# Up products of a split-float MLP: high weights times high and low features in one 512-column matmul

## The reference

```python
def sq_relu_mlp(h, w_up, w_down):
    return jnp.square(jax.nn.relu(h @ w_up)) @ w_down
# x = x + sq_relu_mlp(rms_norm_2(x, norm2_g[l]), w_up[l], w_down[l])
```

## Time and profile before

| | |
|---|---|
| median of 3 runs | 1287.84 us (1287.81 to 1287.95) |
| span of the profiled execution | 1285.7 us; the page gives no other time for it |
| TensorE busy | 1157.5 us, 90% |
| VectorE, ScalarE, GpSimd busy | 71%, 39%, 26% |
| up stage | about 1095 to 1194 us of the span |
| down stage | about 1194 to 1282 us of the span |

### The profile page before, as it was taken

The page is one execution under the profiler, slowest core; times in us unless marked ns, Lnnn a source line. Parts: engine busy times, 40 slices in busy tenths (PEclk is TensorE's granted clock), DMA queues, the critical chain, the costliest instruction groups (busy, mean ns, idle before and its releaser), DMA issues.

```text
span 1285.7 us, 15477 instructions
## 1 busy us (share of the span) xinstructions
PE 1157.5 (90%) x5466; PEld 822.4 (64%) x5466; DVE 911.5 (71%) x1879; ACT 504.7 (39%) x975; POOL 331.6 (26%) x311
## 2 busy tenths in 40 slices
PE   5899999999799998997888888788789999999998
PEld 5888999999755544442333433333335887999787
DVE  6875797788678777776777767677756786666544
ACT  4556544455432223212222122221514577555432
POOL 4000000000245545454444444535441000000000
PEclk9999999999899999999899989988999999999999
DMA  8854377686899999999999999999997523345550
GB/s 361 314 220 174 132 259 282 234 340 251 322 412 423 426 425 425 426 426 426 427 426 427 426 426 426 426 426 427 427 427 307 193 99 118 146 168 190 200 196 34
DMA packets 57697, 405.68 MB, mean 316 GB/s; under 512 B 6908, under 2 KB 7108, under 8 KB 9108
## 3 DMA queue, kind: packets, MB, share of 16 engines
q0 software_dynamic: 38576, 272.49, 50.6%
q1 hardware_dynamic: 19044, 132.19, 27.3%
HBM read 403.61 MB, written 1.05 MB: 315 GB/s over the span
## 4 chain that ended last, share of the span: by engine, by line
PE 47%; DMA 29%; DVE 13%; ACT 6%; issue 3%; POOL 1%; SPq 0%; DVEq 0%; POOLq 0%; ACTq 0%
DMA gbuf<-in_peer_uv,ei 16%; DMA ring<-in_peer_uv,ei 11%; PE bank L822 11%; PE bank L483 5%; PE bank L479 5%; PE bank L480 5%; DVE half L1501 4%; ACT half L1034 3%; PE bank L754 3%; PE bank L1008 2%; PE bank L1010 2%; PE bank L1009 2%; DMA row_place<-in_peer_uv,ei 1%; PE bank L500 1%; PE bank L494 1%
## 5 line engine op out<-in xcount | busy, mean ns | idle before, releaser
L822 PE MATMUL bank<-gbuf,dg 128*128 128x512 f32 x540 | 259.0, 625 | 49.2 <-ACT dg L1313 49.2
L1501 DVE TENSOR_TENSOR half<-ring,half 128x1024 fp32r<-128x1024 f32 x175 | 212.6, 1222 | 112.9 <-ACT half L1034 112.5
L822 PEld LDWEIGHTS bank<-gbuf,dg 128*128 128x128 f32 x540 | 105.1, 199 | 189.8 <-issue 120.3
L1944 DVE CUSTOM_DVE_ANT_0 gbuf<-gbuf,h2t 128x1024 f32<-128x1024 f32 x135 | 165.3, 1225 | 80.5 <-DMA gbuf<-in_peer_uv,ei 79.4
L1034 ACT ACTIVATE half<-ring 128x1024 fp32r<-128x1024 f32 x175 | 183.0, 1052 | 92.4 <-PE bank L1010 45.6
L2289 POOL DMA_INDIRECT gbuf<-in_peer_uv,ei x135 | 160.1, 1186 | 187.1 <-PE bank L822 110.7
L822 PE MATMUL bank<-ring,dg 128*128 128x512 f32 x356 | 171.4, 619 | 26.6 <-ACT dg L1313 26.6
L1305 ACT ACTIVATE za<-za 128x4 f32<-128x4 f32 x62 | 12.7, 205 | 399.6 <-DVE za L1944 399.6
L2289 POOL DMA_INDIRECT ring<-in_peer_uv,ei x89 | 106.8, 1200 | 166.1 <-DVE ei L1917 70.7
L1944 DVE CUSTOM_DVE_ANT_0 ring<-ring,h2t 128x1024 f32<-128x1024 f32 x89 | 108.9, 1225 | 54.7 <-DMA ring<-in_peer_uv,ei 54.7
L822 PEld LDWEIGHTS bank<-ring,dg 128*128 128x128 f32 x356 | 68.7, 196 | 116.6 <-issue 79.0
(11 more groups left out here) (440 smaller groups left out, 1962.2 us busy)
## 6 DMA issues: line engine op xcount, KB each, us to landing
ring<-in_weights SPq DMA_DIRECT2D x114, 1024.0 KB, 4.9
gbuf<-in_weights SPq DMA_DIRECT2D x4, 1024.0 KB, 9.7
gbuf<-in_peer_uv,ei POOLq DMA_INDIRECT x135, 23.2
wq_place<-in_weights SPq DMA_DIRECT2D x2, 1024.0 KB, 6.1
bcs<-in_b_ada POOLq DMA_DIRECT2D x3, 512.0 KB, 9.1
ring<-in_peer_uv,ei POOLq DMA_INDIRECT x89, 22.7
xs<-in_x SPq DMA_DIRECT2D x2, 512.0 KB, 8.4
ya<-in_weights SPq DMA_DIRECT2D x1, 1024.0 KB, 17.2
```

Of the source, the lines that this page charges most:

```text
L822: r = e.matmul(acc[a][j][:, :], dg[:, i % 4, :], expert_rows(i)[:, 1024 + 512 * j:1536 + 512 * j], start=h == 0 and k == 0, stop=h == 7 an ...
L1501: e.tensor_tensor(l, v, h.bitcast(f32), ALU.subtract).then_inc(*o.inc(s_lov, split(n)))
L1944: e.tensor_tensor_reduce(row, row, h2t[:, ITS[n][0], :], 1.0, 0.0, ALU.mult, ALU.add, za[:, n % 2, i % 16:i % 16 + 1]).then_inc(*o.inc(s_d ...
```

## The change

The high and the low features become two planes of one tensor `hf2`, so that both can be streamed behind each other: one matmul of 512 columns writes high x high into columns 0 to 255 of a bank and high x low into columns 256 to 511. The low weights still meet the high features alone, added to columns 0 to 255. All 32 blocks now go through `up_rows`. VectorE adds the two halves of the bank with a reduction over the pair (t, t + 256) and writes the sum to `rl`. ScalarE takes the relu of it in place, in SBUF, and then squares twice: into a new float32 buffer `rq` and, rounded, into `gh`. VectorE's low part is now `rq` minus `gh`. A bank is free after VectorE's sum.

```diff
-    hfh = feats.enter_context(nc.sbuf_tensor("hfh", [128, 8, T], f32r))
-    hfl = feats.enter_context(nc.sbuf_tensor("hfl", [128, 8, T], f32r))
+    hf2 = feats.enter_context(nc.sbuf_tensor("hf2", [128, 2, 8, T], f32r))
...
+    hfh, hfl = hf2[:, 0, :, :], hf2[:, 1, :, :]
...
-        def up_rows(f, g):
-            n = chunk_at["up", f]
+        def up_rows(f, k0, k1):
+
+            n, pb = chunk_at["up", f], banks[f % 4]
             hi, lo = high_done(n)
-            pb = bank(f)
-            for k in range(4 * g, 4 * g + 4):
-                for a in range(2):
-                    e.wait_ge(s_fhi, FHI["h4", 2 * a + g])
-                    e.wait_ge(s_flv, FLV["h4", 2 * a + g])
-                e.matmul(pb[:, 0:256], hi[:, k, :], hfh[:, k, :], start=k == 0, stop=False)
-                e.matmul(pb[:, 0:256], hi[:, k, :], hfl[:, k, :], start=False, stop=False)
+            for k in range(k0, k1):
+                if f < 2:
+                    for a in range(2):
+                        e.wait_ge(s_fhi, FHI["h4", 2 * a + k // 4])
+                        e.wait_ge(s_flv, FLV["h4", 2 * a + k // 4])
+                e.matmul(pb[:, :], hi[:, k, :], hf2[:, :, k, :], start=k == 0, stop=False)
             e.wait_ge(s_lov, split(n))
-            for k in range(4 * g, 4 * g + 4):
+            for k in range(k0, k1):
                 r = e.matmul(pb[:, 0:256], lo[:, k, :], hfh[:, k, :], start=False, stop=k == 7)
             return r
...
         for g in range(2, 32):
-            product("up", g, g % 4, hfh, hfl)
-            frees[g % 4] = ((s_relu, g + 1),)
+            if g < 4:
+                bank(g)
+            else:
+                e.wait_ge(s_usum, g - 3)
+            up_rows(g, 0, 8).then_inc(*o.inc(s_chunk, chunk_at["up", g] + 1))
...
         for g in range(32):
-            taken("up", g)
+            for m in ahead(chunk_at["up", g]):
+                hi(m)
+            e.wait_ge(s_usum, g + 1)
+            e.activation(rl[:, g % 3, :], rl[:, g % 3, :], AF.Relu).then_inc(*o.inc(s_relu, g + 1))
             if g >= 3:
                 e.wait_ge(s_flp, FLP["g", g - 3])
-            e.activation(rl[:, g % 3, :], banks[g % 4][:, 0:256], AF.Relu).then_inc(*o.inc(s_relu, g + 1))
-            e.wait_ge(s_gsq, 5 + g)
-            e.activation(gh[:, g, :], rl[:, g % 3, :], AF.Copy).then_inc(*o.inc(s_fhi, FHI["g", g]))
+            e.wait_ge(s_relu, g + 1)
+            e.activation(rq[:, g % 3, :], rl[:, g % 3, :], AF.Square).then_inc(*o.inc())
+            e.activation(gh[:, g, :], rl[:, g % 3, :], AF.Square).then_inc(*o.inc(s_fhi, FHI["g", g]))
...
-            e.tensor_tensor(gl_[:, g, :], rl[:, g % 3, :], gh[:, g, :].bitcast(f32), ALU.subtract).then_inc(
+            e.tensor_tensor(gl_[:, g, :], rq[:, g % 3, :], gh[:, g, :].bitcast(f32), ALU.subtract).then_inc(
                 *o.inc(s_flp, FLP["g", g]))
...
             lo(chunk_at["up", g] + 2)
-            e.wait_ge(s_relu, g + 1)
-            e.tensor_tensor(rl[:, g % 3, :], rl[:, g % 3, :], rl[:, g % 3, :], ALU.mult).then_inc(*o.inc(s_gsq, 5 + g))
+            if g >= 3:
+                e.wait_ge(s_fhi, FHI["g", g - 3])
+            e.wait_ge(s_chunk, chunk_at["up", g] + 1)
+            e.tensor_reduce(rl[:, g % 3, :], banks[g % 4][:, :].rearrange("p (j t) -> p t j", j=2), AX.X, ALU.add).then_inc(
+                *o.inc(s_usum, g + 1))
             if g:
                 square_lo(g - 1)
```

More of the change, by code:

```diff
@@ L173, in build_program @@
         "a2", "lru_in", "gl", "lru_mul", "g_sq", "xo", "neg_max", "norm_bcast_read", "h2_done", "h_gained", "rstd_diag", "first_experts")]
+    s_usum = sem("s_up_sum")
     s_pool, s_flp, s_id, s_const, s_wbd, s_iu = [sem("s_" + n) for n in (
@@ L351, in build_program @@
     rl = st("rl", [128, 3, T])
+    rq = st("rq", [128, 3, T])
     stage.close()
     ctx.push(feats)
+    hfh, hfl = hf2[:, 0, :, :], hf2[:, 1, :, :]
     bada, n1pre, ca_w, cqk_w = pc0[:, 8:56], pc0[:, 56:64], pc0[:, 64:88], pc0[:, 88:120]
@@ L970, in tensor_program @@
                 frees[2 * c + a] = ((s_gsq, 2 * c + a + 1),)
-        def up_rows(f, g):
-            n = chunk_at["up", f]
+        def up_rows(f, k0, k1):
+            n, pb = chunk_at["up", f], banks[f % 4]
             hi, lo = high_done(n)
-            pb = bank(f)
-            for k in range(4 * g, 4 * g + 4):
-                for a in range(2):
-                    e.wait_ge(s_fhi, FHI["h4", 2 * a + g])
-                    e.wait_ge(s_flv, FLV["h4", 2 * a + g])
-                e.matmul(pb[:, 0:256], hi[:, k, :], hfh[:, k, :], start=k == 0, stop=False)
-                e.matmul(pb[:, 0:256], hi[:, k, :], hfl[:, k, :], start=False, stop=False)
+            for k in range(k0, k1):
[4 more added lines that the diff above has]
+                e.matmul(pb[:, :], hi[:, k, :], hf2[:, :, k, :], start=k == 0, stop=False)
             e.wait_ge(s_lov, split(n))
-            for k in range(4 * g, 4 * g + 4):
+            for k in range(k0, k1):
                 r = e.matmul(pb[:, 0:256], lo[:, k, :], hfh[:, k, :], start=False, stop=k == 7)
             return r
-        up_rows(0, 0)
+        bank(0)
+        up_rows(0, 0, 4)
         for a in range(2):
             tokens_columns(a, 1)
-        up_rows(1, 0)
+        bank(1)
+        up_rows(1, 0, 4)
         for f in range(2):
-            up_rows(f, 1).then_inc(*o.inc(s_chunk, chunk_at["up", f] + 1))
-            frees[f] = ((s_relu, f + 1),)
+            up_rows(f, 4, 8).then_inc(*o.inc(s_chunk, chunk_at["up", f] + 1))
         for g in range(2, 32):
-            product("up", g, g % 4, hfh, hfl)
-            frees[g % 4] = ((s_relu, g + 1),)
+            if g < 4:
[3 more added lines that the diff above has]
+            up_rows(g, 0, 8).then_inc(*o.inc(s_chunk, chunk_at["up", g] + 1))
         accs = [bank(4 + i) for i in range(4)]
```

## The result

The changed kernel takes 1322.14 us (median of 4 runs, 1321.73 to 1322.32), the one before 1287.89 beside it: ratio 1.0267, 95% interval 1.0255 to 1.028. The forecast was 1321.3 us, in a range from 1315 to 1330.

What follows compares the result with a forecast made beforehand. The prediction took the ScalarE-VectorE ring, not TensorE, to bound the up stage: 31 x 1.06 + 0.6 = 33.5 us, and 1285.7 + 33.5 + 2.1 = 1321.3 us, 2.6% slower, range 1315 to 1330.

Steps and rivals of the forecast that it cites:

- the ring: Up stage, ScalarE and VectorE waiting on each other through splits, sum, relu and squares: 4.05 us a block, before 2.99.
- TensorE sets the pace after all: Rival, up stage: TensorE bounds it, a block goes from 2.99 to 2.8 us, 1282 us in all; chance 0.03.
- TensorE's saving is off the path: Up stage: wider matmuls make TensorE's block 2.8 us, saving at most 3 us, none of it on the path.
- The sum: VectorE's reduction of a bank's two halves, up stage: 0.69 us, time going with the 512 floats read.
- both rivals on it (0.42, 1.23): Sum priced by its 256 results, 0.42 us, 1312.7 us, chance 0.04; strided sum dear, 1.23 us, 1338.6 us, chance 0.08.
- Squares: ScalarE's Square to rq and Square to gh in the up stage: 0.33 us each from start to next start.
- Relu and its wait: ScalarE's relu from SBUF and the wait for its own result, up stage: 0.45 us together, moved into the ring.
- The start: First sum to next high split at the stage's start: 1.83 us in place of 1.20, so 0.6 us later.
- The rows decided rightly: Trace rows, against the skill page's clock swings (some 5 us over): TensorE idling 1.25 us a block hardly costs.
- the clock did not fall for good: Rival, up stage: TensorE stays at the 1.2 GHz level, 5.6 us a block, +81 us, 1369 us; chance 0.02.
- the rival in which Square needs its own table: ScalarE, up stage: two table loads a block at 1.283 us each, +82 us, 1403 us; chance 0.01.
- Around the span: Time between the profiled span of 1285.7 us and the median of 1287.84 us: 2.1 us, kept unchanged.

Runs made afterwards that it cites:

- square_first: The kernel before, with VectorE's square of block g ahead of its low split of chunk g+2: 1283.31 us, ratio 0.9972.
- narrow: The changed kernel with two 256-column matmuls into both halves of the bank in place of the 512-column one: 1321.24 us, ratio 1.0261.
- low_wide: The changed kernel with the low weights also meeting high and low features in 512-column matmuls: 1322.09 us, ratio 1.0271.
- sum_first: The changed kernel with VectorE's sum of block g's bank halves before the low split of chunk g+2: 1279.66 us, ratio 0.9944.
- own_wait_first: The changed kernel with ScalarE's two waits before the first square swapped, its own relu first, then block g-3's low part: 1319.67 us, ratio 1.0241.

## Why the prediction was right

- *Who sets the pace.* Before the change it was ScalarE and VectorE in their ring, with TensorE 0.11 us a block faster: square_first opened the ring and won 4.3 us, where 3.5 were expected. The rival "TensorE sets the pace after all" is false.
- *TensorE's saving is off the path.* narrow and low_wide moved TensorE's block to 2.88 and 3.62 us without an effect (both times as seen with the ring open). I had 2.8 us for the new block; sum_first shows 2.79.
- *The ring.* Forecast 4.05, measured 4.070. The sum took 0.684 (0.69 taken) and both rivals on it (0.42, 1.23) fall. Squares 0.32 and 0.31 for 0.33. Relu and its wait 0.45 in the first blocks, as taken from the earlier trace rows, but 0.51 from block 3 on: this is the one term of the ring that was mis-sized, and own_wait_first shows the second wait as its cause. The prediction's list of ScalarE's work leaves this wait (for the low part of block g-3) out. The shorter squares hide 0.03 of its 0.06.
- *The start.* Forecast 0.6, measured 0.85. From the first sum to the next high split it takes 1.80 us (1104.44 to 1106.24), where 1.83 were taken, against 1.20 before: these are the 0.6. The other 0.25 are that the sum began later than the relu had begun before (1104.19), in an execution that was already 0.39 late at the high split of block 2. In the traces of the other runs that split begins anywhere from 1100.3 to 1103.9, so this part is no effect that the runs show of the change. In all 33.39 + 0.85 + 0.06 behind the loop = 34.3 us, for 33.5.
- *Room and clock.* TensorE idled 1 us a block and was granted the full clock all the same. The rows decided rightly, and the clock did not fall for good either. What the Trainium skill tells of another kernel (page "TensorE: Matmul & The Clock Gate", section "A second HAM failure mode: psum-queue depth-cycling"), that such micro-idling swings the clock, did not come true here: the granted clock was 1.00 from 1106 to 1180.
- *Tables.* Between 1095 and 1240 the trace has no table load on ScalarE, so the rival in which Square needs its own table is false.
- *Around the span.* The profiled execution took 1321.73 us with a span of 1320.0: 1.7 us, not the 2.1 taken. That the forecast and the median are only 0.8 us apart is in part luck: the forecast has 0.5 us too little in the ring, 0.3 too little at its ends and 0.4 too much outside the span, while the median lies 0.4 above the profiled execution; and the runs of the kernel before beside the experiments differ by up to 4.0 us (1285.3 to 1289.3). The mechanism and the 1.08 us a block don't rest on that.

The largest single finding was outside the forecast: the loss hangs on the place of one statement. The version with the sum first beats both kernels, at 0.994 of the one before in both measurements.

## What to carry to other kernels

Before pricing an edit, follow the ring: from one engine's instruction through every "stands behind" and "waits for" until it closes, and add start-to-start distances; a saving outside it is worth nothing and an operation moved into it costs its full start-to-start time each turn (here 0.45 to 0.51 us for the relu). An engine that consumes another's result and also prepares that one's next operand should do the consuming first; here that one swap was worth 42 us. A busy share near 100% doesn't prove the pace: see whether the engine's first instruction of a block starts when something else lands.

## What was not expected of the hardware

Where two waits stand ahead of an operation of ScalarE, the second in the program is an instruction of its own in the queue (the 29 event instructions of line 1497 in the changed kernel). If it is the one that decides, 0.06 us are added (0.51 instead of 0.45 from relu to square); if the deciding wait stands first, nothing is. A chain of waits shows such an instruction in the ring; this is the turn in the changed kernel from 1150 on:

```profile
1149.79 0.43 ACT rl L1494
1150.22 0.02 issue
1150.24 0.02 ACTq L1497
1150.26 0.04 issue
1150.30 0.07 ACT rq L1498
```

Also, a reduction over pairs that stand 256 floats apart in a bank took 0.684 us for 512 floats read, about as much as one over contiguous floats in SBUF (0.680, line 2068 in the earlier trace rows).
